# Weight products that read the moving operand alternately from its two halves

## The reference

```python
x = first_block(x, ...)      # three mixers (GLA, pooling, MoBA) behind one w_in, w_branch_*, w_out, then a SwiGLU FFN
x = second_block(x, mem, ...)
# second_block:
x = x + 0.5 * swiglu(rmsnorm(x), gate, up, down)
x = x + hybrid_mixer(rmsnorm(x), w_in, ...)          # NSA and forgetting attention, gates, w_up_*, w_out
x = x + memory_cross_attention(rmsnorm(x), rmsnorm(mem), w_q, w_kv, w_o)
x = x + 0.5 * swiglu(rmsnorm(x), gate, up, down)
return rmsnorm(x)
```

## Time and profile before

| | |
|---|---|
| median of 3 runs | 1101.3 us (1101.09 to 1101.75) |
| span of the profiled execution | 1100.8 us |
| TensorE busy | 1087.9 us, 7530 matmul records |
| VectorE busy | 719.8 us |
| ScalarE busy | 555.3 us |
| HBM over the span | 192 GB/s |

### The profile page before, as it was taken

The page is one execution under the profiler, slowest core; times in us unless marked ns, Lnnn a source line. Parts: engine busy times, 40 slices in busy tenths (PEclk is TensorE's granted clock), DMA queues, the critical chain, the costliest instruction groups (busy, mean ns, idle before and its releaser), DMA issues.

```text
span 1100.8 us, 18185 instructions
## 1 busy us (share of the span) xinstructions
PE 1087.9 (99%) x7530; PEld 981.1 (89%) x7530; DVE 719.8 (65%) x1085; ACT 555.3 (50%) x840; POOL 30.3 (3%) x49
## 2 busy tenths in 40 slices
PE   9999999999999999999999999999999999999997
PEld 8898878889999988899999889887788989999985
DVE  5687665877666645656666545867767657666653
ACT  6643575545444544544454445646644446445442
POOL 0000500000000000000000001000000000000000
PEclk9999999999999999999999999999999999999999
DMA  7654545655665665576686559534365445565662
GB/s 265 231 173 159 192 148 198 225 188 175 193 204 185 221 200 182 192 248 211 233 274 207 174 186 321 185 113 128 122 235 173 148 133 188 189 202 190 196 203 77
DMA packets 63821, 211.01 MB, mean 192 GB/s; under 512 B 7451, under 2 KB 14803, under 8 KB 62844
## 3 DMA queue, kind: packets, MB, share of 16 engines
q1 hardware_dynamic: 63452, 209.57, 57.6%
q10 hardware_dynamic: 288, 0.29, 0.1%
HBM read 206.41 MB, written 5.27 MB: 192 GB/s over the span
## 4 chain that ended last, share of the span: by engine, by line
PE 85%; DVE 6%; ACT 4%; DMA 3%; issue 1%; POOL 0%; SPq 0%; POOLq 0%; ACTq 0%; DVEq 0%
PE ps L869 13%; PE ps L872 13%; PE ps L871 13%; PE ps L861 12%; PE ps L863 12%; PE ps L862 12%; DMA raw<-in_wflat 3%; DVE wlo L1652 1%; PE ps L911 1%; ACT whi L1313 1%; PE ps L1043 1%; PE ps L958 1%; ACT m_Pb L1463 1%; PE ps L1029 1%; PE ps L1234 1%
## 5 line engine op out<-in xcount | busy, mean ns | idle before, releaser
L869 PE MATMUL ps<-hT_hi,whi_b 128*128 128x256 f32 x1344 | 373.7, 278 | 0.5 <-DVE wlo_b L1652 0.5
L871 PE MATMUL ps<-hT_hi,wlo_b 128*128 128x256 f32 x1344 | 371.2, 276 | 0.0
L872 PE MATMUL ps<-hT_lo,whi_b 128*128 128x256 f32 x1344 | 371.2, 276 | 0.0
L1652 DVE TENSOR_TENSOR wlo<-raw,whi 128x1024 fp32r<-128x1024 f32 x176 | 215.4, 1240 | 113.7 <-ACT whi L1313 112.9
L1652 DVE TENSOR_TENSOR wlo_b<-raw,whi_b 128x1024 fp32r<-128x1024 f32 (+1 forms) x186 | 217.4, 1189 | 106.2 <-ACT whi_b L1313 105.9
L869 PEld LDWEIGHTS ps<-hT_hi,whi_b 128*128 128x128 f32 x1344 | 252.3, 188 | 3.7 <-issue 2.3
L871 PEld LDWEIGHTS ps<-hT_hi,wlo_b 128*128 128x128 f32 x1344 | 252.3, 188 | 0.3
L872 PEld LDWEIGHTS ps<-hT_lo,whi_b 128*128 128x128 f32 x1344 | 252.3, 188 | 0.0
L1313 ACT ACTIVATE whi<-raw 128x1024 fp32r<-128x1024 f32 x176 | 181.9, 1057 | 110.4 <-PE ps L863 89.1
L1313 ACT ACTIVATE whi_b<-raw 128x1024 fp32r<-128x1024 f32 (+1 forms) x186 | 183.2, 1024 | 32.4 <-PE ps L863 15.3
L861 PE MATMUL ps<-whi,hT_hi 128*128 128x512 f32 (+1 forms) x256 | 101.8, 398 | 1.6 <-DVE wlo L1652 1.6
(11 more groups left out here) (338 smaller groups left out, 1317.6 us busy)
## 6 DMA issues: line engine op xcount, KB each, us to landing
raw<-in_wflat SPq DMA_DIRECT2D x355, 512.0 KB, 4.0
wide<-scratch SPq DMA_DIRECT2D x1, 2048.0 KB, 11.2
m_w<-in_cmp_k_w SPq DMA_DIRECT2D x4, 512.0 KB, 6.1
m_w<-in_cmp_v_w SPq DMA_DIRECT2D x4, 512.0 KB, 6.1
m_alibi<-in_c_alibi SPq DMA_DIRECT2D x1, 1536.0 KB, 6.6
m_xT<-in_xT SPq DMA_DIRECT2D x4, 256.0 KB, 5.6
x<-in_x SPq DMA_DIRECT2D x2, 512.0 KB, 8.9
m_memT<-in_memT SPq DMA_DIRECT2D x1, 1024.0 KB, 5.9
```

The lines of the kernel that those rows point to most:

```text
L869: e.matmul(o, hi[:, k, c], xs.h(k0 + k), start=first and k == 0 and f % 2 == 0, stop=False, skip_group_check=True)
L871: e.matmul(o, lo[:, k, c], xs.h(k0 + k), start=False, stop=False, skip_group_check=True)
L872: r = e.matmul(o, hi[:, k, c], xs.l(k0 + k), start=False, stop=last and k == kt - 1, skip_group_check=True)
L1652: e.tensor_tensor(slot(wlo, u)[:, w], raw[u % NRAW][:, w], slot(whi, u)[:, w].bitcast(F32), ALU.subtract).then_inc(*w_lo.did(u, c))
```

## The change

Three helpers are new. `in_turn` gives a moving operand with `n` columns in the order 0, n/2, 1, n/2 + 1, and so on: one column from the first half, one from the second. It is put around the moving operand of every product of kinds "a", "b" and "s". No matmul is added, removed or moved.

For kind "a" the columns of the weights are laid out on the host so that this order yields the old one: even columns first, then odd ones. For kinds "b" and "s" the results stand in PSUM with the tokens 0, 128, 1, 129 and so on. `in_order` reads them with a step of two elements (8 bytes) and the evictions write them in the old order. `split_tokens` gives the other operands the same shape. Where an eviction also scales (`scalar_tensor_tensor`, which has room for fewer dimensions), it becomes two instructions of 256 elements; where the scale is 1 it becomes a `tensor_tensor`.

```diff
+        def in_turn(ap):
+            return ap.rearrange("p (a b) -> p b a", a=2)
+        def split_tokens(ap):
+            return ap.rearrange("p i (a j) -> p i a j", a=2)
+        def in_order(bank):
+            return bank.rearrange("p (i j a) -> p i a j", a=2, j=128)
...
-                            e.matmul(o, xh, hi[:, k, :], start=first and k == 0, stop=False)
-                            e.matmul(o, xh, lo[:, k, :], start=False, stop=False)
-                            r = e.matmul(o, xl, hi[:, k, :], start=False, stop=last and k == kt - 1)
+                            e.matmul(o, xh, in_turn(hi[:, k, :]), start=first and k == 0, stop=False)
+                            e.matmul(o, xh, in_turn(lo[:, k, :]), start=False, stop=False)
+                            r = e.matmul(o, xl, in_turn(hi[:, k, :]), start=False, stop=last and k == kt - 1)
...
-                            e.matmul(o, lo[:, k, c], xs.h(k0 + k), start=False, stop=False, skip_group_check=True)
+                            e.matmul(o, lo[:, k, c], in_turn(xs.h(k0 + k)), start=False, stop=False, skip_group_check=True)
...
-                    e.scalar_tensor_tensor(out=out[:, 2 * i:2 * i + 2, :], in0=p2, scalar=scale if name != "qk" or i == 1 else 1.0,
-                                           in1=m.wide(), op0=ALU.mult, op1=ALU.mult).then_inc(*ps.emptied(name, i))
+                    if scale == 1.0 or name == "qk" and i == 0:
+                        r = e.tensor_tensor(o, p2, m.wide(), ALU.mult)
+                    else:
+                        for f in range(2):
+                            r = e.scalar_tensor_tensor(out=o[:, f], in0=p2[:, f], scalar=scale, in1=m.wide()[:, f],
+                                                       op0=ALU.mult, op1=ALU.mult)
+                    r.then_inc(*ps.emptied(name, i))
...
-                    p2 = ps.tile(f"f{i}gu{c}", j)[:, :].rearrange("p (i t) -> p i t", i=2)
+                    p2 = in_order(ps.tile(f"f{i}gu{c}", j)[:, :])
...
-                    e.tensor_tensor((sg, hh)[j][c % 2][:, :, :], p2, m.wide(),
+                    e.tensor_tensor(split_tokens((sg, hh)[j][c % 2][:, :, :]), p2, m.wide(),
...
+        if PRODUCTS[name][0] == "a":
+            w = np.concatenate([w[:, 0::2], w[:, 1::2]], 1)
```

More of the change, by code:

```diff
@@ L698, in wide @@
             def wide(self, p=128, n=2):
-                return self.rT[0:p, :].unsqueeze(1).to_broadcast([p, n, T])
+                return split_tokens(self.rT[0:p, :].unsqueeze(1).to_broadcast([p, n, T]))
         def on_bank(tag):
@@ L842, in unit @@
                             c = slice(128 * f, 128 * f + 128)
-                            e.matmul(o, hi[:, k, c], xs.h(k0 + k), start=first and k == 0 and f % 2 == 0, stop=False,
+                            e.matmul(o, hi[:, k, c], in_turn(xs.h(k0 + k)), start=first and k == 0 and f % 2 == 0, stop=False,
                                      skip_group_check=True)
-                            e.matmul(o, lo[:, k, c], xs.h(k0 + k), start=False, stop=False, skip_group_check=True)
-                            r = e.matmul(o, hi[:, k, c], xs.l(k0 + k), start=False, stop=last and k == kt - 1,
+                            e.matmul(o, lo[:, k, c], in_turn(xs.h(k0 + k)), start=False, stop=False, skip_group_check=True)
+                            r = e.matmul(o, hi[:, k, c], in_turn(xs.l(k0 + k)), start=False, stop=last and k == kt - 1,
                                          skip_group_check=True)
@@ L876, in unit @@
                     for k in range(kt):
-                        e.matmul(o, hi[:, k, :], xs.h(k), start=k == 0, stop=False)
-                        e.matmul(o, lo[:, k, :], xs.h(k), start=False, stop=False)
-                        r = e.matmul(o, hi[:, k, :], xs.l(k), start=False, stop=k == kt - 1)
+                        e.matmul(o, hi[:, k, :], in_turn(xs.h(k)), start=k == 0, stop=False)
+                        e.matmul(o, lo[:, k, :], in_turn(xs.h(k)), start=False, stop=False)
+                        r = e.matmul(o, hi[:, k, :], in_turn(xs.l(k)), start=False, stop=k == kt - 1)
                 if name != "f2dn1" or j < len(ids) - 2:
@@ L891, in of @@
                         xl = xs.l(kv + k)[:, t * 128:t * 128 + 128]
-                        e.matmul(o, xh, h[:, k, :], start=False, stop=False)
-                        e.matmul(o, xh, l[:, k, :], start=False, stop=False)
-                        r = e.matmul(o, xl, h[:, k, :], start=False, stop=v == u and j == last and k == kt - 1)
+                        e.matmul(o, xh, in_turn(h[:, k, :]), start=False, stop=False)
+                        e.matmul(o, xh, in_turn(l[:, k, :]), start=False, stop=False)
+                        r = e.matmul(o, xl, in_turn(h[:, k, :]), start=False, stop=v == u and j == last and k == kt - 1)
                     return r
@@ L1717, in kept @@
                 for i in range(n):
-                    p2 = ps.tile(name, i)[:, :].rearrange("p (i t) -> p i t", i=2)
+                    p2, o = in_order(ps.tile(name, i)[:, :]), split_tokens(out[:, 2 * i:2 * i + 2, :])
                     q.wait_ge(*used.at(ends[name]))
                     q.wait_ge(*ps.out("across", m.i))
-                    e.scalar_tensor_tensor(out=out[:, 2 * i:2 * i + 2, :], in0=p2, scalar=scale if name != "qk" or i == 1 else 1.0,
-                                           in1=m.wide(), op0=ALU.mult, op1=ALU.mult).then_inc(*ps.emptied(name, i))
+                    if scale == 1.0 or name == "qk" and i == 0:
[5 more added lines that the diff above has]
+                    r.then_inc(*ps.emptied(name, i))
             def few(name, n, out):
@@ L1727, in few @@
                 q.wait_ge(*ps.out("across", m.i))
-                e.tensor_tensor(out[0:n, :], ps.tile(name, 0)[0:n, 0:T], m.rT[0:n, :],
+                e.tensor_tensor(split_tokens(out[0:n, :].unsqueeze(1)), in_order(ps.tile(name, 0)[0:n, 0:T]), m.wide(n, 1),
                                 ALU.mult).then_inc(*ps.emptied(name, 0))
@@ L1741, in out_pu @@
                 for i in range(2):
-                    p2 = ps.tile("pu", i)[:, :].rearrange("p (i t) -> p i t", i=2)
+                    p2 = in_order(ps.tile("pu", i)[:, :])
                     q.wait_ge(*used.at(ends["pu"]))
                     q.wait_ge(*ps.out("across", 0))
-                    e.tensor_tensor(pu[:, 2 * i:2 * i + 2, 16:272], p2, norms[0].wide(),
+                    e.tensor_tensor(split_tokens(pu[:, 2 * i:2 * i + 2, 16:272]), p2, norms[0].wide(),
                                     ALU.mult).then_inc(*ps.emptied("pu", i))
@@ L2144, in out_kv @@
                 q.wait_ge(*ps.out("across", 3))
-                e.tensor_tensor(kvs[:, :, :], ps.tile("kv", 0)[:, :].rearrange("p (i t) -> p i t", i=2), norms[3].wide(),
+                e.tensor_tensor(split_tokens(kvs[:, :, :]), in_order(ps.tile("kv", 0)[:, :]), norms[3].wide(),
                                 ALU.mult).then_inc(*ps.emptied("kv", 0))
@@ L2165, in out_ksw @@
             def out_ksw():
-                p2 = ps.tile("ksw", 0)[:, :].rearrange("p (i t) -> p i t", i=2)
+                p2 = in_order(ps.tile("ksw", 0)[:, :])
                 q.wait_ge(*used.at(ends["ksw"]))
                 q.wait_ge(*ps.out("across", 3))
-                e.tensor_tensor(ksw[:, :, :], p2, norms[3].wide(), ALU.mult).then_inc(*ps.emptied("ksw", 0))
+                e.tensor_tensor(split_tokens(ksw[:, :, :]), p2, norms[3].wide(), ALU.mult).then_inc(*ps.emptied("ksw", 0))
             def mem_head(h):
```

## The result

The changed kernel takes 1075.1 us (median of 4 runs, 1072.89 to 1075.85); the kernel before took 1101.2 us on the same chip (4 runs, 1100.64 to 1101.75). The ratio is 0.9756, with a 95% interval of 0.974 to 0.9772. The profiled execution has a span of 1073.9 us, 26.9 less than before.

A forecast was written before the change was run, and what follows sets the result against it. The prediction took TensorE's moving columns as the bound: 1100.8 - 36.5 (faster moving reads) + 4 (evictions) = 1068.3 us of span, so 1069 us. The range was 1056 to 1112 us, leaving out the case of a fetch for each column.

The forecast's parts named there:

- What bounds the kernel: Whole kernel: TensorE is busy 1087.9 of 1100.8 us, so time is nearly moving columns times the time of one.
- The lost cycle is in the read of the moving operand, and reading in turn removes it: TensorE weight products: one cycle in 17 is lost reading moving columns; the change was taken to save 36.5 us.
- The term of 19.7 us: Kind "a" on the chain: 403 us times 4.9%, as 512-column matmuls fall to 215.6 ns.
- 109 ns for kind "b": Kind "b" matmuls of 256 columns: 113.3 ns falls to 109 ns, 3.8% less, the weight load not counting.
- The term of 16.8 us: Kind "b" on the chain: 441 us times 3.8%, as 256-column matmuls fall to 109 ns.
- Nothing better is possible: Weight products: 36.5 us is the most that this number of columns allows the change to save.
- Evictions +4 us: Evictions of kinds "b" and "s" where tasks wait for heads: stepped PSUM reads and extra halves cost 0 to 8 us.
- T1: Moving read's reason for the gain: the turn from one 64-byte block to the next hides behind the second stream.
- Each column is a fetch of its own: Rival for the moving read: each column fetched afresh, 1974, 3118 or about 3980 us; chance 0.20.
- The Trainium skill's rule of 16-byte lines: SBUF reads: a different line at each access is penalised; the change does that at every access; no size given.
- The distance between the halves: Halves lie 512 and 1024 bytes apart; the kinds parting would prove the forecast wrong; no row tells if distance matters.
- T3: Post-prediction theory: the moving read has two lanes, even and odd accesses, each needing successive accesses to the same 16 bytes.

The follow-up runs named there:

- e1: Changed kernel with only the moving weights of kind "a" read in turn, the rest as before the change: 1082.62 us, ratio 0.9821 to the kernel before.
- e2: Changed kernel with only kinds "b" and "s" read in turn, with the reordered evictions, kind "a" contiguous: 1093.72 us, ratio 0.9922 to the kernel before.
- e8: Changed kernel with kind "a" moving weights read in pairs by turns from the two halves (0, 1, n/2, n/2 + 1): 1313.0 us.
- e5: Changed kernel with kind "a" moving weights read in steps of 8 bytes, all even positions, then all odd: 1565.9 us.
- e12: Changed kernel with kind "a" halves still read in turn, but in steps of two columns within each half: 1094.26 us.
- e6: Changed kernel with kind "a" moving weights read in steps of 64 bytes (0, 16, 32, ...): 1525.3 us.
- e13: Changed kernel with kind "a" halves still read in turn, but in steps of four columns (16 bytes) within each half: 1564.44 us.
- e7: Changed kernel with kind "a" moving weights read by turns from four quarters in place of two halves: 1206.0 us.
- e3: Changed kernel with both split-weight buffers moved to 256 bytes past a multiple of 512: 1074.67 us, ratio 0.9747 to the kernel before.
- e4: Changed kernel with both split-weight buffers at a multiple of 512 bytes, like the moving features: 1074.24 us in one run.
- e9: Changed kernel with 64 stationary columns in place of 128 in the second of kind "b"'s three matmuls, the other 64 results' correction omitted: 1073.8 us.
- e11: Changed kernel with kind "b" stationary weights loaded from columns 8 bytes apart instead of side by side: 1101.6 us, ratio 1.0001 to the kernel before.

## Why the prediction was right, and where its working was off

- *What bounds the kernel* held. Fewer nanoseconds per matmul came out almost one for one: 2088 matmuls with 512 columns at 10.9 ns less are 22.8 us, 4416 with 256 columns at 1.6 ns less (48 of them of kind "a" at about 8) some 7.4; TensorE's busy time fell by 31.9 and the span by 26.9. The prediction counted only what lies on the chain, 85 to 87% of the matmuls. The trace shows the discount as 5.0 us more idle time, of which 2.8 are waits for VectorE's split of the weights.
- *The lost cycle is in the read of the moving operand, and reading in turn removes it* held: 226.7 to 215.9 ns for kind "a", and for kind "s" with 16 columns 113 to 109 (the three matmuls of the earlier trace rows are among the fastest; its distances before run from 113 to 119). The term of 19.7 us measured 19.1 in e1. The step to it was weaker than it looked: "it grows with the columns" compared kind "b" with kind "a", and within kind "a" 256 and 512 columns stand almost equally far above columns over clock (12.7 and 13.4 ns). The term came out all the same, since it rests on the rows of kind "a" itself.
- *109 ns for kind "b"* is the term that was mis-sized. It took the earlier trace rows, where 16 stationary columns ran at 113 ns like 128, as a sign that the load does not count. At 113.3 ns the contiguous moving read covered whatever comes with 128 stationary columns, most likely their load; at 109 it is covered no more, and 111.7 is the floor. The term of 16.8 us becomes 441 x 1.6 / 113.3 = 6.2 by the same method, and e2 measured 8.0. "Nothing better is possible" was right, but the best case was out of reach.
- *Evictions +4 us* (0 to 8): the step in PSUM costs nothing (691 ns before and after), the extra halves 1.6 us of VectorE, and e2's gain of 8.0 us (6.5 to 10.8 by its interval) is no less than the matmuls of kinds "b" and "s" account for (4368 x 1.64 ns = 7.2). No cost shows; the term is 0 as far as that interval can tell.
- *Sum*: 1100.8 - 19.7 - 6.2 + 0 = 1074.9 of span, against 1073.9. The forecast of 1068.3 was 5.6 us low because the missing 10.6 us of kind "b" outweighed the 4 us of the evictions; that two errors of opposite sign met brought it nearer than its terms were.
- *Why it would be so* (T1) was wrong, though it gave the right number for kinds "a" and "s"; so far as the reason goes, that was luck. e8 goes against it, and e5 by its price. e12 shows that a second stream as such brings nothing: two streams, and no gain at all.
- *"Each column is a fetch of its own"* was a real danger, only not of this order: e5, e6 and e13 run at 0.84 to 0.88 ns per column, where the prediction had taken the float32 row's 0.84, and end at 1525 to 1566 us with kind "a" alone changed. The rows of VectorE were the wrong analogue on either side.
- *The Trainium skill's rule of 16-byte lines* ("Advanced Engine Details and Errata", Memory Cachelines: at least two hits on a line in succession) was read as speaking against the change. The runs agree with its 16 bytes and its "at least two" if successive accesses are counted within each of two lanes: e13 and e12 differ only in one hit against two and stand at 451 and 226.7 ns. e7 and e8, one hit each, are slower than contiguous, as the rule has it, but by less. By the rule read over all accesses in one row e5, which hits each line twice in succession, would be fast; it is at 451.
- *The distance between the halves* (512 or 1024 bytes) made no difference that shows: kinds "s" and "a" both reached the forecast pace. Nor did the offset of the buffers (e3, e4). No variant beat the changed kernel; the 1074.67, 1074.24 and 1073.8 us of e3, e4 and e9 lie within its range.

**What stays open.** T3 is a model that sorts six of the eight orders, two of them by forecast; no run shows the lanes themselves. Taken at its word it is wrong on e7 (283 ns) and e8 (333 ns), where a lane changes between two lines at every access yet pays less than in e5. Nor does it say why exactly two hits lose one cycle in 17, or why a contiguous read loses 6.7 ns in kind "b" and 12.7 in kind "a" at 256 columns. What holds reads in turn at 111.7 ns with 128 stationary columns is open between their load and the used width of the array.

## What to carry to other kernels

When TensorE runs back to back in a four-byte type, compare the distance between starts with columns over clock. Here all but 2.6 of the 13.4 ns of rest at 512 columns lay in the read of the moving operand, and reading its two halves in turn, with the layout prepared outside the kernel, removed it for nothing. To tell a loss per column from one per instruction, compare two lengths within one kind of product. Make such a change by halves and one column at a time: quarters, pairs or a step of 8 bytes took 1.25 to 2 times the contiguous time. Before counting on a faster stream, ask what was hidden under the slow one: here matmuls with 128 stationary columns met a floor 2.7 ns above the forecast, and the order of the columns in their load is worth as much as the whole gain.

## What the hardware showed unexpectedly

- The moving read in fp32r, ns for 512 columns: 215.9 halves in turn, 226.7 contiguous and halves in turn in steps of 8 bytes, 283 quarters, 333 pairs, 433 and 451 in steps of 64 and of 8 bytes, 451 halves in turn in steps of 16 bytes.
- Matmuls of 256 columns read in turn run at 109 ns with 16 to 64 stationary columns, at 111.7 with 128, and at 118.8 with 128 loaded from 8 bytes apart, though the load's record grows by only 5 ns (192 to 197). The Trainium skill ("TensorE: Matmul & The Clock Gate", LDWEIGHTS) gives columns / 1.2 ns, 106.7 ns for 128; as an estimate from that figure, the load would still have been hidden under 109.
- In e9 and e11 the distance to the next matmul follows the stationary columns of the matmul that starts it, not the load that runs beside it (109.1 ns after 64 columns with a full load beside it, 111.6 after 128 with a load of 64).
- A contiguous read of 256 columns took 119.4 ns in kind "a" and 113.3 in kind "b", in turn 111.7 in both; placing the stationary buffers of kind "b" 0 or 256 bytes past a multiple of 512 changed nothing for reads in turn (e3, e4).
- VectorE reads PSUM in steps of 8 bytes at full pace.
